# Norms by tile, expert 0's rows by a one-hot product, and latent attention by head pairs with values stationary

## The reference, cut to what matters

```python
def diff_attention(q, k, v, lam, subln_g, lambda_init, cos, sin):
...
        s = jnp.einsum('bhmqd,bhmkd->bhmqk', qb, k).astype(jnp.float32) * scale
        p = jax.nn.softmax(s, axis=-1)
        w = p[:, :, 0] - lam * p[:, :, 1]
        return jnp.einsum('bhqk,bhke->bhqe', w.astype(v.dtype), v)
...
    o = rms_norm(o, subln_g) * (1.0 - lambda_init)
...
def latent_attention(c_q, c_kv, k_r, q_norm_g, w_uq, kv_norm_g, w_ukv, cos, sin):
...
        s = (jnp.einsum('bhqd,bhkd->bhqk', qn, k_nope)
             + jnp.einsum('bhqr,bkr->bhqk', qr, k_rope)).astype(jnp.float32) * scale
        p = jax.nn.softmax(s, axis=-1)
        return jnp.einsum('bhqk,bhke->bhqe', p.astype(v.dtype), v)
...
    return jnp.concatenate([a_out, b_out], axis=-1) @ w_o
...
        x = layer_norm(DN_ALPHA * x + m, ln1_g[i], ln1_b[i])
        f = hier_moe(x, w_router_group[i], b_router_group[i], w_router_expert[i], b_router_expert[i],
                     w_gate[i], w_up[i], w_down[i])
        x = layer_norm(DN_ALPHA * x + f, ln2_g[i], ln2_b[i])
```

## Time and profile before

| | |
|---|---|
| median of 3 runs | 3281.58 us (3279.41 to 3287.19) |
| the profiled execution: time, span | 3288.22 us, 3286.4 us |
| mean granted clock of TensorE | 0.981 |
| PE busy | 3130.5 us, 95% |
| PE weight loads | 2391.3 us, 73% |
| DVE, ACT, POOL busy | 2154.1 us (66%), 1599.9 us (49%), 391.3 us (12%) |
| chain that ended last | PE 80%, DVE 7%, DMA 5%, ACT 4%, issue 3%, POOL 1% |
| moved by DMA | 599.20 MB, mean 182 GB/s |

### The profile page before, as it was taken

One profiled execution on the slowest core, in us unless ns is written; L12 is line 12 of the kernel. 1 busy time (PEld: TensorE's weight loads), 2 busy tenths in 40 slices (PEclk: granted clock), 3 DMA queues, 4 the chain that ended last, 5 costly groups with the idle time before them and its releaser, 6 DMA issues.

```text
span 3286.4 us, 39211 instructions
## 1 busy us (share of the span) xinstructions
PE 3130.5 (95%) x14815; PEld 2391.3 (73%) x14815; DVE 2154.1 (66%) x2300; ACT 1599.9 (49%) x1905; POOL 391.3 (12%) x274
## 2 busy tenths in 40 slices
PE   8889899999999989899999989997899999999998
PEld 7567677777766867567777757877788887778886
DVE  2365588888874366688888865564477745757653
ACT  2474277777764353477777753342321213722211
POOL 0000222222212000322222220010000000000000
PEclk9999999999999999999999999998999999999999
DMA  6300489999983212699999972420123223223321
GB/s 237 135 1 14 189 337 361 356 354 364 353 330 111 81 37 114 247 351 349 361 354 363 358 261 64 85 53 1 64 91 103 83 97 103 77 84 103 103 103 64
DMA packets 174479, 599.20 MB, mean 182 GB/s; under 512 B 25571, under 2 KB 74899, under 8 KB 124947
## 3 DMA queue, kind: packets, MB, share of 16 engines
q1 hardware_dynamic: 140528, 541.75, 45.0%
q0 software_dynamic: 23472, 51.42, 4.4%
q10 hardware_dynamic: 10355, 4.33, 0.5%
HBM read 581.17 MB, written 48.23 MB: 192 GB/s over the span
## 4 chain that ended last, share of the span: by engine, by line
PE 80%; DVE 7%; DMA 5%; ACT 4%; issue 3%; POOL 1%; DVEq 0%; SPq 0%; ACTq 0%; POOLq 0%
PE bank L1828 20%; PE bank L1830 20%; PE bank L1829 20%; PE bank L1840 3%; DMA ring<-w_gate 2%; PE bank L2376 2%; PE bank L1892 2%; PE bank L1893 2%; PE bank L2126 1%; PE bank L1835 1%; PE bank L1836 1%; PE bank L1953 1%; PE bank L2157 1%; PE bank L1929 1%; ACT ring_rounded L1284 1%
## 5 line engine op out<-in xcount | busy, mean ns | idle before, releaser
L1829 PE MATMUL bank<-ring_rounded,big_rounded 128*96 128x512 f32 (+1 forms) x1680 | 661.0, 393 | 0.0
L3020 DVE TENSOR_TENSOR ring_rounded<-ring,big_rounded 128x2048 fp32r<-128x2048 f32 x252 | 567.5, 2288 | 37.2 <-ACT big_rounded L1284 35.6
L2674 DVE TENSOR_TENSOR ring_rounded<-ring,ring_rounded 128x2048 fp32r<-128x2048 f32 (+2 forms) x124 | 273.5, 2248 | 404.4 <-ACT ring_rounded L1096 404.2
L1284 ACT ACTIVATE big_rounded<-ring 128x2048 fp32r<-128x2048 f32 x252 | 478.5, 1918 | 59.1 <-DMA ring<-w_up 48.2
L1096 ACT ACTIVATE ring_rounded<-ring 128x2048 fp32r<-128x2048 f32 (+2 forms) x124 | 226.6, 1877 | 459.1 <-DMA ring<-ffn_w_down 163.9
L1828 PE MATMUL bank<-big_rounded 128*96 128x512 f32 x992 | 394.6, 398 | 0.5 <-DVE ring_rounded L3020 0.5
L3020 DVE TENSOR_TENSOR ring_rounded<-ring,ring_rounded 128x2048 fp32r<-128x2048 f32 x128 | 292.8, 2289 | 155.1 <-ACT ring_rounded L1284 146.5
L1830 PE MATMUL bank<-big_rounded,XH_rounded 128*96 128x512 f32 x992 | 392.2, 395 | 0.0
L1829 PEld LDWEIGHTS bank<-ring_rounded,big_rounded 128*96 128x96 f32 (+1 forms) x1680 | 277.8, 165 | 106.1
L1284 ACT ACTIVATE ring_rounded<-ring 128x2048 fp32r<-128x2048 f32 x128 | 245.1, 1916 | 220.6 <-DMA ring<-w_gate 220.5
L1830 PE MATMUL bank<-ring_rounded,XH_rounded 128*96 128x512 f32 (+1 forms) x776 | 309.0, 398 | 0.0
(11 more groups left out here) (462 smaller groups left out, 5214.6 us busy)
## 6 DMA issues: line engine op xcount, KB each, us to landing
ring<-w_up SPq DMA_DIRECT2D x128, 1024.0 KB, 7.6
ring<-w_down SPq DMA_DIRECT2D x128, 1024.0 KB, 7.9
ring<-w_gate SPq DMA_DIRECT2D x128, 1024.0 KB, 7.1
ring<-ffn_w_up SPq DMA_DIRECT2D x44, 1024.0 KB, 6.5
ring<-ffn_w_down SPq DMA_DIRECT2D x10, 2048.0 KB, 7.8
ring<-ret_gdn_w_in SPq DMA_DIRECT2D x8, 2048.0 KB, 12.9
expert_rows<-lnp POOLq DMA_DIRECT2D x1, 12288.0 KB, 40.9
ring<-odd_w_qkv SPq DMA_DIRECT2D x6, 2048.0 KB, 8.0
```

Source lines behind the costliest of these rows:

```text
L1284: act.activation(one_pass(expert_hi(j)), expert_raw(j), ACT.Copy).then_inc(signal("half_rounded").sem, 1)
L1829: pe.matmul(dst, x_hi, y_lo, start=False, stop=False)
L2674: dve.tensor_tensor(one_pass(w), w, parts(hi(c)[:, ks, :]), ALU.subtract).then_inc(split[c.pair], 1)
L3020: dve.tensor_tensor(one_pass(expert_raw(j)), expert_raw(j), parts(expert_hi(j)), ALU.subtract).then_inc(signal("half_split").sem, 1)
```

## The change

It has four parts.

- **A's loop** is a function of its own, `two_maps`, without the waits of ACT and DVE for their own results after each instruction. PE's wait for B's rotated rows (`rope_b`) moves from before A to the end of A, where B's first transposes now stand.
- **B's loop** (`head_pairs`) has 16 steps of two heads. Scores and transposes are the same in number and shape. DVE multiplies the weights themselves by the reciprocal, two operations of 512 columns a step, before they are turned. In the product the values are now stationary (64 columns) and the turned weights move (128 columns), so the outcome lies with features on partitions and needs no turn. A's norm, the remainder of the first chunk of `w_o` and the turn of A's four blocks are done inside this loop. `keep_warm` of 14 and the turn of 32 are gone.
- **Expert 0's rows** come from `first_rows`: DVE marks for each token which of 96 places it takes among expert 0's rows (three more operations in `place`), and PE multiplies X's columns (stationary) with these marks, 16 products of 96 columns for each half of the tokens. `keep_warm` of 4, the 15 products and the gather for expert 0 are gone. In `up_first` the whole parts with gate's and up's weights come first, and the remainders after.
- **Norms of blocks 2 and 3** go by tile: the part that ends turns each normed tile between its last products, and the first three column groups of the next part are done for the first two tiles while the last two are normed (`first_T_by_halves`). Gains are multiplied in by DVE. The `keep_warm` of 3, 10 and 3 are gone, the output is stored by tile, and the feed-forward part's second weights come in chunks of 3, 3, 4, 4, 4, 4 blocks in place of 4, 4, 4, 4, 4, 2.

The diff, cut to its core:

```diff
@@ PE, first mixer @@
+                def weighted(i):
+                    g, t = divmod(i, T)
+                    v = U["o0_T"][KD // 2 + g]
...
+                    for m in range(2):
+                        for c in range(T):
+                            ins = pe.matmul(ps(v)[B_V * m:B_V * (m + 1), t * P:(t + 1) * P], E["VB"][:, c, 2 * g + m, :], B_["WT"][:, i % 2, m, c, :],
+                                            start=(c == 0), stop=(c == T - 1))
...
+                for i in range(n + 3):
+                    if i < n:
+                        scores(i)
+                        if i % T == 2 and i // T + 1 < PAIRS:
+                            pair_qk(i // T + 1)
+                    if i == n:
+                        pe.wait_ge(signal("a_normed").sem, signal("a_normed").next(pe))
+                        turn_normed(0)
+                        turn_normed(1)
+                    if 2 <= i < n + 2:
+                        turn_weights(i - 2)
+                    if i == n + 1:
+                        turn_normed(2)
+                        turn_normed(3)
+                    if i >= 3:
+                        weighted(i - 3)
@@ DVE, first mixer @@
+            def head_pairs():
...
+                    if i >= 1:
+                        sum_factors(u, i - 1)
+                        for m in range(2):
+                            p, j = E["p"][(i - 1) % 3][:, m, :], 2 * (i - 1) + m
+                            ins = dve.tensor_scalar(p, p, rcp[:, j:j + 1], None, ALU.mult)
+                        ins.then_inc(signal("p_scaled").sem, 1)
+                    if 1 <= i < 1 + T:
+                        subln_squares(i - 1)
+                    if i in (6, 11):
+                        rest_of_half_of(W["even_o"][0], i // 11)
+                    if 7 <= i < 7 + T:
+                        subln_scaled(i - 7)
+                    if i >= 8 and i % T == 0:
+                        rest_of_pair(i // T - 2)
@@ PE, after the first attention @@
-                attention("A")
-                attention("B")
-                keep_warm(U["o0_T"][0], 14)
-                pe.wait_ge(signal("a_normed").sem, signal("a_normed").next(pe))
...
-                turn("o0_T", XH, None)
+                two_maps()
+                head_pairs()
@@ PE, routing @@
             def positions(l, q):
                 u = U[f"route{l}"][2 + q]
-                if q == 0:
-                    keep_warm(u, 4)
                 pe.wait_ge(signal("chosen").sem, signal("chosen").next(pe))
...
+            def first_rows(l, q):
+                pe.wait_ge(signal("first_marked").sem, signal("first_marked").next(pe))
+                for b in range(2):
...
+                    for t in (2 * q, 2 * q + 1):
+                        x = X[:, t, :].rearrange("c (h p k) -> c h k p", h=2, k=4)
+                        for j in range(4):
+                            ins = pe.matmul(psum[b][:, j * CAP:(j + 1) * CAP], x[:, b, j, :], M["sel"][:, t, :],
+                                            start=(t == 0 and j == 0), stop=(t == T - 1 and j == 3))
...
-                positions(l, 0)
-                positions(l, 1)
+                for q in range(2):
+                    positions(l, q)
+                    first_rows(l, q)
@@ PE, feed-forward parts @@
+            def first_T_by_halves(c, us, tiles, name):
...
+                for half in range(2):
+                    for t in (2 * half, 2 * half + 1):
+                        turned_tile(name, t)
...
+                    for q, (u, m) in enumerate(zip(us[0:3], tiles)):
...
+                        if half == 0 and q == 1:
+                            turn_tile(name, XH, T - 1, "xh_ready")
...
-                linear_chunk(W["mix_out"][1], U["mix_out"][1])
+                for t in range(T):
+                    linear_chunk(W["mix_out"][1], U["mix_out"][1], tiles=(t,))
+                    if t:
+                        turn_tile("rmsf0_T", XH, t - 1, "xh_ready")
...
-                keep_warm(U["rmsf0_T"][0], 3)
-                turn("rmsf0_T", XH, "xh_ready")
@@ SP @@
-            sp.dma_start(out[0].rearrange("(t p) d -> p t d", p=P), XH[:, :, :]).then_inc(signal("out_stored").sem, 16)
+            for t in range(T):
+                sp.wait_ge(signal("out_ready").sem, signal("out_ready").next(sp))
+                sp.dma_start(out[0][t * P:(t + 1) * P, :], XH[:, t, :]).then_inc(signal("out_stored").sem, 16)
```

691 lines of the change are left out of this document (414 added, 277 removed).

## The result

Four runs of the changed kernel have a median of 3231.6 us (3225.1 to 3234.1); against the kernel before on the same chip the ratio is 0.983 (0.981 to 0.985), some 56 us faster. Run again later, with the kernel before beside it, it gave 0.982 (0.980 to 0.983). Forecast were 75 us, so the sign was right and a quarter of the gain did not come: by the ratio the forecast's 3207 became some 3225, outside its own range of 3196 to 3220 and inside the wide one, 3193 to 3230. The profiled execution took 3234.1 us, span 3232.3, against 3288.2 and 3286.4 before: 54 less. I go through it place by place.

The account below looks back on a forecast made before the run. PE was taken as the bound, busy for 95% of the span, some of it with unread products. Attention -38, expert 0 -15.5 and norms -21.6 made -75: 3281.6 to 3207 us, own range 3196 to 3220, wide range 3193 to 3230.

Parts of the forecast that it names:

- Attention, -38: Attention: A's loop -4, B's loop -17, the gap between B and w_o -19, with 2 us given back for collisions.
- old pace: Rival, B's loop: products with values stationary are no faster than before, 8.3 us less gain, 3215 us; chance 0.14.
- Expert 0, -15.5: Expert 0's start, both layers: gate's next load 9.5 us earlier in each, less 3.5 for the clock; bounds 0 and -20.
- nothing at expert 0: Rival, expert 0: new products run at 1.2 GHz and the next load meets others; 15.5 us lost, 3222 us; chance 0.12.
- Norms, -21.6: Norms by tile: -3.5 before each feed-forward part, -9.6 into the recurrent mixer, -5 at the end; bounds -12 and -27.
- lock: Rival, norms: POOL's power of a late tile and DVE's remainder wait for each other; 13.5 us lost, 3220 us; chance 0.06.
- Slower: Rival, B's loop and expert 0: without unread products the clock falls to 1.2 GHz for long; +16, 3298 us; chance 0.02.

Follow-up runs that it names:

- gate_first: Changed kernel with expert 0's gate products, remainders included, complete before up's; ratio 0.978 (0.976 to 0.980) to the kernel before the change.
- rows_in_order: Changed kernel with expert 0's row products reading X's columns side by side, not at a stride of four; ratio 0.977 (0.975 to 0.979) to the kernel before.
- old_start: Changed kernel with the routing and expert 0 put back as before the change; ratio 0.981 (0.980 to 0.983) to the kernel before.

## Why the prediction was right and where it failed

**Attention, -38: measured -39.2.** Right in sum by luck: the parts were others. A gave 9 where I had 4, over the upper bound of 8. DVE's step was sized well: 2.54 us where it doesn't wait (178.38 to 180.92), 0.21 less than before, for the 0.2 allowed. The rest I did not have. Of A's 6 us 2.5 came in its first four steps, over which the clock was at half in the trace of before and full in that of after; 0.8 of the start was won earlier. Whether before's other executions had that low clock too, no trace shows.

B's loop gave 10.3 and not 17. The step that failed is "a step of two heads is then 2 x 0.91 + 2 x 0.44 + 2 x 0.59 = 3.88": it was 4.30, near the 4.40 of the rival "old pace". For that rival I had noted that in rows 4 the load was half as wide "and the pace followed". It did not. Record by record, the products of one head start 0.109 apart with 64 stationary columns (246.039, 246.148, 246.257), and 0.112 apart before with 128. What made rows 4 fast is that the products of its two heads, which write different halves of the partitions, run beside each other: one starts at 1193.380, the other at 1193.393. There a head has four records, here eight, and the second head's first starts (246.372) with the first head's fifth (246.366), so that only half of them overlap: 1.51 for sixteen. The gap before w_o is gone whole: 20.0 us for the 19 forecast. PE as the bound of the loop held; with DVE's scaling cut away w_o began only 0.4 us earlier.

**Expert 0, -15.5: measured -3.1 in the first trace** (1.0 and 2.0 from the logits to the fifth expert), and by ratio not faster than the old start. The step that failed is "as X is read at a stride of four, which no row shows, I take 3.9": it is 7.8. That alone would be 3.9 a layer. Two things hang on it that the sum did not have: the first product stands on PE until 337.6, 1.6 after the second choice is ready; and the clock stays at half, so that the first whole parts cost 0.43. A third fault has another cause, the order in `up_first`: the gate's loads are issued 1.9 us ahead of up's and not 5.6, and up's last load then took 12.5 us. The sum took "the rest of the way, load, rounding, split" as unchanged. With side-by-side columns up's loads still came late, and with gate_first's order alone they did not. I had this as the rival "nothing at expert 0" (0.12), with the right place and half the cause: its "the next load meets others" came true. Its other half, the clock, doesn't slow the row products; it slows what comes behind them. In the changed kernel it fell as they began, and it fell there with side-by-side columns too, so that only its long stay at half goes with the stride.

So time won ahead of the loads was lost again at them: the second expert's rows were turned 2.9 us earlier after P than before (33.9 for 36.8), the third's no longer (55.8 for 55.6). Time by which the loads themselves came earlier did arrive, in gate_first and rows_in_order. The loop that follows moves 6.5 MB an expert with the DMA engines busy for 0.92 to 0.93 of it, and PE for 0.985 to 0.992, so that neither alone can be called its bound (busy times by stretch, columns as in the earlier trace rows; the changed kernel's first loop):

```profile
422.00:923.30 501.30, 493.81 (x2269) 353.46 (x2268) 419.16 (x271) 374.42 (x324) 136.27 (x53) 1.00 0.92 352
```

And that of old_start:

```profile
424.70:920.00 495.30, 491.33 (x2269) 352.61 (x2268) 419.27 (x271) 374.49 (x324) 114.28 (x53) 1.00 0.93 357
```

Time times rate is the same, some 176 MB, as it must be for the same weights. What counts at the start is when its loads begin, and how many ask at once.

**The loops, not in the sum: +8.7 in the first trace** (7.4 and 1.3). Over the fourteen profiles in the table one is from 493.6 to 502.0. The four with the old start lie at 493.9 to 496.7; of twenty-four with the new one five are no longer than that. Whether the new start costs some 3 us a layer there, or this is scatter, stays open; I made no experiment that holds the start and changes the loop. The four terms together are -52.7; the last 1.4 us lie scattered between the marks.

**Norms, -21.6: measured -19.1.** The three places gave 3.7, 9.7 and 3.2 (forecast 3.5, 9.6 and 3.5), the end 2.5 and not 5. The step that failed is "the store of 2 MB took 6.6, one of 512 KB 3.3: -3.3". The 3.3 was a load's row; the store took 2.6, but it no longer ends last: POOL's drain, which had ended 0.2 before the old store, still took 7.7, so the end went from 7.0 to 6.8. What was won is on POOL: its last two operations took 1.27 and 1.59 beside DVE's scalings, and take 0.19 and 0.54 with DVE idle, 2.1 us of the 2.5.

The rival "lock" was right in its mechanism and wrong in its price. Into the recurrent mixer, DVE's row and POOL's:

```profile
2697.16 2.29 DVE L2919 TENSOR_TENSOR ring_rounded<-ring,ring_rounded 128x2048 fp32r<-128x2048 f32 x1
2698.53 0.97 POOL L933 TENSOR_SCALAR st<-st 128x1 f32<-128x1 f32 x1 [4.68 <-ACT lnp L1437]
```

The operation that takes 0.19 elsewhere took 0.97 and ended 0.05 after the remainder. At the other two places it was 0.85 and 0.62, ended the same way, always in the second tile. The powers themselves met no remainder of weights and took 0.54 to 0.57, also in the fourth tile, where DVE read a PSUM bank beside them. So it costs under a microsecond at each place where the rival had 4.5, and it falls on the second tile, whose norm the products cover: PE's wait there is 0.42. The Trainium skill, SBUF — State Buffer, section "SBUF: two separate sides", has the shared port pair as an exclusive lock for a whole instruction. The trace agrees, here and at the end of the kernel before.

For 256 columns the line through two rows (0.121) was near to the 0.120 measured. The Trainium skill, TensorE: Matmul & The Clock Gate, section "Back-to-back issue gap", gives 109 ns; the trace is 10% slower.

**Slower** fell in B's loop: the clock was 1.00 over it without any unread product. At expert 0 the clock was at half for 24 and 27 us (330.3 to 354.2, and 1279.2 to 1306.5 in the second layer), where it had been for 10 and 7.

## What to carry to other kernels

Price a product by both its sides as they lie in memory: a stationary side read at a stride can set the pace, and a moving side's length then says nothing. Before a price is taken from a row, see whether its products run beside each other, and whether yours would. Ahead of a stage that loads set, time won is worth only what it brings forward the first loads; put the work that frees a buffer first, and free buffers one after another. Where two things end together, shortening one of them gives nothing: look at every engine's end, its drain too. Unread products that fill a wait are not the cost they seem: taking them out gives nothing unless what follows can start.

## What the runs showed of the hardware

- A load of 128 stationary columns in fp32 took 192 ns at full clock and 333 ns at half with columns side by side, and 329 ns at either clock at a stride of four (16 bytes). The records were 0.112 and 0.213 us apart side by side, 0.233 at the stride. ACT's copy of 1,024 columns read at that stride took 1.96 us. The gathered rows' turn reads 96 rows at the same stride with loads of 218 ns; it has one record for each turn, where a row product has two. Why its loads are so much shorter was not tried.
- The clock was granted at 0.50 over the strided products, though PE was busy throughout (5.00 of 5.00 us). With the same products read side by side it was at 0.50 over part of the first (328.5 to 331.9) and at 1.00 from then on.
- Matmuls of the same form (64 stationary, 128 moving columns) took 0.074 us each in runs of 8, 0.094 in runs of 16 and 0.078 in one of 32. Within one head they were 0.109 apart everywhere; those of two heads, writing different halves of the partitions, ran beside each other, four records of each in all these runs.
- A POOL operation on 128x1 that began during a DVE remainder of weights (2.29 us) ended 0.05 us after it: 0.62 to 0.97 us in place of 0.19.
- The end of the program took 6.7 to 7.0 us after the last scaling, whether 2 MB, 512 KB or 64 KB were left to store. POOL's drain began 0.2 us behind its last power, took 7.6 to 7.75 us in all three, and ended 0.2 to 0.6 us ahead of the span's end.
- Two loads of the gate's and two of up's weights, 1 MB each, asked for within 2.3 us, had the last land after 12.5 us; with 5.6 us between the pairs it was 8.4.
